# A decoder layer with a mixture of experts: the low parts of the turned rows by a matmul with minus the identity and a ScalarE copy

## What is computed

```python
def moe_ffn(h, w_router, b_router, w_gu, b_gu, w_dn, b_dn):
    ...
    logits = (xf @ w_router + b_router).astype(jnp.float32)
    top_v, top_e = lax.top_k(logits, TOP_K)
    gates = jax.nn.softmax(top_v, axis=-1)
    ...
    def expert_block(args):
        xe, e = args
        gu = xe @ w_gu[e] + b_gu[e]
        gate = jnp.minimum(gu[..., 0::2], SWIGLU_LIMIT)
        up = jnp.clip(gu[..., 1::2], -SWIGLU_LIMIT, SWIGLU_LIMIT)
        act = (up + 1.0) * (gate * jax.nn.sigmoid(gate * SWIGLU_ALPHA))
        return act @ w_dn[e] + b_dn[e]
    ...
    out = jnp.zeros((t, d), jnp.float32).at[row_tok].add(
        yb.reshape(n_rows, d).astype(jnp.float32) * row_gate[:, None])
```

## Time and profile before

| what | us |
| --- | --- |
| median of 3 runs | 1427.1 |
| lowest and highest | 1425.9, 1428.12 |
| the profiled execution, its own time | 1428.16 |
| its span in the profile | 1426.5 |
| busy in the span: PE, DVE, ACT | 1331.1, 1276.3, 1026.1 |

### The profile page before, as it was taken

How to read it: one execution, slowest core, us unless ns; L and a number is a source line. 1 busy time by engine, 2 the same in 40 slices (tenths; PEclk the granted TensorE clock), 3 DMA queues, 4 the chain that set the end, 5 groups by cost and what they waited for, 6 DMA issues and landing times.

```text
span 1426.5 us, 20070 instructions
## 1 busy us (share of the span) xinstructions
PE 1331.1 (93%) x6410; PEld 1058.9 (74%) x6410; DVE 1276.3 (89%) x1246; ACT 1026.1 (72%) x945; POOL 439.6 (31%) x286
## 2 busy tenths in 40 slices
PE   6999989898999999999999999999999999999996
PEld 5876866776877777787877777777878777788883
DVE  7448665689999999999999999999999999999998
ACT  5344444447788888878788888888787888877772
POOL 0000000023143536253444435362535444311100
PEclk9999999999999999999999999999999999999998
DMA  9511130279999999999999999999999999999994
GB/s 352 192 59 60 35 133 31 83 264 382 378 395 403 402 393 406 409 403 405 406 406 400 402 394 404 397 401 406 403 398 400 408 397 396 390 380 374 364 372 178
DMA packets 85573, 472.83 MB, mean 331 GB/s; under 512 B 16619, under 2 KB 16659, under 8 KB 34336
## 3 DMA queue, kind: packets, MB, share of 16 engines
q1 hardware_dynamic: 70736, 451.79, 79.6%
q0 software_dynamic: 14800, 20.55, 4.1%
HBM read 467.80 MB, written 22.02 MB: 343 GB/s over the span
## 4 chain that ended last, share of the span: by engine, by line
PE 50%; DVE 22%; issue 13%; DMA 7%; ACT 6%; POOL 0%; DVEq 0%; SPq 0%; POOLq 0%; ACTq 0%
DVE w_lo L1004 11%; PE gu_bank L1536 10%; PE gu_bank L1538 9%; PE gu_bank L1537 9%; DMA raw<-in_w_down_dram 5%; ACT w_hi L645 4%; PE turn_bank L1536 3%; PE turn_bank L1537 3%; PE turn_bank L1538 3%; DVE arena L1384 2%; PE bank L1536 1%; PE bank L1538 1%; PE bank L1537 1%; PE bank L1861 1%; DVE arena L1394 1%
## 5 line engine op out<-in xcount | busy, mean ns | idle before, releaser
L1004 DVE TENSOR_TENSOR w_lo<-raw,w_hi 128x2048 fp32r<-128x2048 f32 x409 | 916.4, 2283 | 61.1 <-ACT w_hi L645 60.1
L645 ACT ACTIVATE w_hi<-raw 128x2048 fp32r<-128x2048 f32 x409 | 771.9, 1921 | 120.7 <-PE gu_bank L1538 96.2
L610 POOL DMA_INDIRECT expert_rows<-arena x32 | 215.9, 6747 | 303.7 <-ACT arena L831 147.7
L1536 PE MATMUL gu_bank<-w_hi,turned 128*128 128x512 f32 x624 | 246.6, 395 | 3.8 <-DVE w_lo L1004 3.7
L1538 PE MATMUL gu_bank<-w_hi,turned 128*128 128x512 f32 x624 | 243.3, 390 | 0.0
L1537 PE MATMUL gu_bank<-w_lo,turned 128*128 128x512 f32 x624 | 243.1, 390 | 0.0
L1542 PE MATMUL gu_bank<-w_hi,turned 128*128 128x512 f32 x448 | 180.0, 402 | 29.2 <-DVE w_lo L1004 27.9
L1543 PE MATMUL gu_bank<-w_lo,turned 128*128 128x512 f32 x448 | 175.1, 391 | 0.0
L1536 PEld LDWEIGHTS gu_bank<-w_hi,turned 128*128 128x128 f32 x624 | 117.2, 188 | 33.6 <-DVE w_lo L1004 6.6
L584 POOL COPY arena<-arena 128x1 int32 (+1 forms) x32 | 53.0, 1657 | 285.7 <-PE bank L1854 275.1
L1538 PEld LDWEIGHTS gu_bank<-w_hi,turned 128*128 128x128 f32 x624 | 117.1, 188 | 24.8
(11 more groups left out here) (343 smaller groups left out, 1786.4 us busy)
## 6 DMA issues: line engine op xcount, KB each, us to landing
raw<-in_w_gate_up_dram SPq DMA_DIRECT2D x264, 1024.0 KB, 9.5
raw<-in_w_down_dram SPq DMA_DIRECT2D x132, 1024.0 KB, 8.4
raw<-in_w_in_dram SPq DMA_DIRECT2D x10, 1024.0 KB, 7.2
raw<-in_w_out_dram SPq DMA_DIRECT2D x4, 1024.0 KB, 5.1
raw<-expert_rows SPq DMA_DIRECT2D x4, 1024.0 KB, 6.5
turned<-split_biases POOLq DMA_DIRECT2D x132, 4.0 KB, 6.7
raw<-in_w_mem_kv_dram SPq DMA_DIRECT2D x2, 1024.0 KB, 12.5
arena<-in_x_dram SPq DMA_DIRECT2D x1, 2048.0 KB, 13.9
```

The lines of the kernel that those rows point to most:

```text
L610: pool.indirect_dma_start(y_dram, bass.IndirectOffsetOnAxis(idx_scatter, 0), y_row, None, bounds_check=TOPK * S - 1, oob_is_err=False).the ...
L645: a.activation(home, raw_ap, ACT.Copy).then_inc(hi_ready, halves)
L1004: v.tensor_tensor(home[1], raw_ap, home[0].bitcast(F32), ALU.subtract).then_inc(lo_ready, halves)
L1536: pe.matmul(bank, a[0], b[0], start=first, stop=False)
```

## The change

Only iterations W and N change, that is the 14 pairs. PE no longer leaves the turned rows in PSUM as they are. Once ACT has copied the high parts out, PE multiplies them with minus the identity and adds the result in PSUM, so that the low parts stand there (`rest_of_x`, `rest_of_acts`, two matmuls each). ACT then copies them out (`low_x`, `low_act`, two instructions each), and the four pairs of subtractions leave DVE. `rest_of_acts` stands between g3 and g4 on PE, `rest_of_x` between d0 and d1 (in N behind `fold_gate_up`). On ACT `low_act` stands behind one more `hi_m` after `turn_act`, and `low_x` behind one more `hi_m` after `turn_x`. The transposes of both kinds are now written as matmuls that clear a bank only at its first piece. `wide_after_wide` and the last iteration keep the subtractions on DVE.

```diff
@@ ACT @@
+            def low_x(n, rows=P):
+
+                low = lx[:, :, :] if rows == P else hx[:, :, NARROW_ROWS:P]
+                a.wait_ge(x_rest, n)
+                for q in range(2):
+                    ks = slice(4 * q, 4 * q + 4)
+                    a.activation(low[:, ks, :], turned_rows[:, ks, 0:rows], ACT.Copy).then_inc(xlo_ready, 1)
+
+            def low_act(n, rows=P):
+
+                low = la[:, :, :] if rows == P else ha[:, :, NARROW_ROWS:P]
+                a.wait_ge(act_rest, n)
+                for q in range(2):
+                    ks = slice(4 * q, 4 * q + 4)
+                    a.activation(low[:, ks, :], turned_rows[:, ks, 0:rows], ACT.Copy).then_inc(alo_ready, 1)
...
+            a.activation(minus_one, ident, ACT.Copy, scale=-1.0)
...
                 turn_act_narrow(0, b)
                 turn_act_narrow(1, b)
-                for i in range(7, 12):
+                hi_m(GU + 7, b)
+                low_act(b, NARROW_ROWS)
+                for i in range(8, 12):
                     hi_m(GU + i, b)
...
-                for i in range(12, 16):
+                hi_m(GU + 12, b)
+                low_x(b, NARROW_ROWS if narrow_next else P)
+                for i in range(13, 16):
                     hi_m(GU + i, b)
                 low_of_down(b * 12 + (16 + GU))
...
                 turn_act(0, b)
                 turn_act(1, b)
-                for i in range(7, 11):
+                hi_m(GU + 7, b)
+                low_act(b)
+                for i in range(8, 11):
                     hi_m(GU + i, b)
...
                 hi_m(GU + 12, b)
+                low_x(b)
                 sigmoid(b + 1, NARROW_ROWS)
@@ DVE @@
                     lo_m(GU + i, b)
-                turn_act(0, b * 2)
-                turn_act(1, b * 2 + 1)
                 for i in range(7, 12):
                     lo_m(GU + i, b)
-                turn_x(0, b * 2 + 3)
-                turn_x(1, b * 2 + 4)
                 clamp(b + 1, folded)
@@ PE @@
+            def rest_of_x(n, rows=P):
+
+                pe.wait_ge(xhi_ready, n * 2 + 4)
+                for q in range(2):
+                    ks = slice(4 * q, 4 * q + 4)
+                    ins = pe.matmul(turned_rows[:, ks, 0:rows], minus_one, hx[:, ks, 0:rows], start=False, stop=True,
+                                    skip_group_check=True)
+                ins.then_inc(x_rest, 1)
+
+            def rest_of_acts(n, rows=P):
+
+                pe.wait_ge(ahi_ready, n * 2 + 1)
+                for q in range(2):
+                    ks = slice(4 * q, 4 * q + 4)
+                    ins = pe.matmul(turned_rows[:, ks, 0:rows], minus_one, ha[:, ks, 0:rows], start=False, stop=True,
+                                    skip_group_check=True)
+                ins.then_inc(act_rest, 1)
...
                     if k == 2:
                         turn_acts(b)
+                    if k == 3:
+                        rest_of_acts(b)
...
                     if j == 0:
                         fold_gate_up(n)
+                        rest_of_x(b)
```

More of the change, by code:

```diff
@@ L283, in hymba_layer @@
         ha, la = (R[:, i * D:(i + 1) * D].rearrange("p (k s) -> p k s", k=KT) for i in (2, 3))
+        minus_one = R[:, 7 * D:7 * D + P]
         ones_r = R[:, 7 * D + P:7 * D + 2 * P]
@@ L321, in hymba_layer @@
         x_kept = sem("x_kept")
+        x_rest, act_rest = sem("x_rest"), sem("act_rest")
         ones_ready, bias_saved, bias_now_in = sem("ones_ready"), sem("bias_saved"), sem("bias_now_in")
@@ L1368, in turn_x_narrow @@
                                 high.bitcast(F32), ALU.subtract).then_inc(xlo_ready, 1)
[L1370 to L1374, removed]
             def clamp(n, folded=None):
@@ L1439, in wide_after_wide, with wide_after_narrow @@
                     lo_m(GU + i, b)
-            def wide_after_narrow(b, narrow_next):
+            def wide_after_narrow(b):
                 for i in range(4, 7):
                     lo_m(GU + i, b)
-                turn_act_narrow(0, b * 2)
-                turn_act_narrow(1, b * 2 + 1)
                 for i in range(7, 11):
@@ L1450, in wide_after_narrow @@
                 lo_m(GU + 11, b)
[L1451 to L1455, removed]
                 activate(b + 1, b)
@@ L1477, in _ @@
             with v.Fori(1, NARROW) as n:
-                wide_after_narrow(n * 2, True)
+                wide_after_narrow(n * 2)
                 narrow_after_wide(n * 2 + 1, n + 1)
-            wide_after_narrow(LOOP_FROM - 2, False)
+            wide_after_narrow(LOOP_FROM - 2)
             wide_after_wide(LOOP_FROM - 1)
@@ L1853, in turn_rows @@
                 for k in range(KT):
-                    ins = pe.transpose(psum[6 + k // 4][:, k % 4 * P:(k % 4 + 1) * P],
-                                       h_row[:, k * P:(k + 1) * P], ident)
+                    ins = pe.matmul(psum[6 + k // 4][:, k % 4 * P:(k % 4 + 1) * P], h_row[:, k * P:(k + 1) * P], ident,
+                                    start=k % 4 == 0, stop=True, is_transpose=True, skip_group_check=True)
                 ins.then_inc(xtp_done, 1)
+            def rest_of_x(n, rows=P):
[12 more added lines that the diff above has]
+                ins.then_inc(act_rest, 1)
             def turn_acts(n):
@@ L1860, in turn_acts @@
                 for k in range(KT):
-                    ins = pe.transpose(psum[6 + k // 4][:, k % 4 * P:(k % 4 + 1) * P],
-                                       act_by_slice[:, k, :], ident)
+                    ins = pe.matmul(psum[6 + k // 4][:, k % 4 * P:(k % 4 + 1) * P], act_by_slice[:, k, :], ident,
+                                    start=k % 4 == 0, stop=True, is_transpose=True, skip_group_check=True)
                 ins.then_inc(atp_done, 1)
@@ L1909, in wide_after_wide, with wide_after_narrow @@
                     down(j, 2 * GU + j, b)
-            def wide_after_narrow(b):
+            def wide_after_narrow(b, rows_next=NARROW_ROWS):
                 pe.wait_ge(sig_ready, b)
@@ L1918, in wide_after_narrow @@
                         turn_acts(b)
+                    if k == 3:
+                        rest_of_acts(b, NARROW_ROWS)
                 gu_bias(b)
@@ L1924, in wide_after_narrow @@
                     down(j, 2 * GU + j, b, narrow=True)
+                    if j == 0:
+                        rest_of_x(b, rows_next)
             def narrow_after_wide(b, n, between=None):
@@ L1950, in _ @@
                 narrow_after_wide(b, n + 1)
-            wide_after_narrow(LOOP_FROM - 2)
+            wide_after_narrow(LOOP_FROM - 2, P)
             wide_after_wide(LOOP_FROM - 1, NARROW)
```

## The result

| kernel | median us | runs | ratio to the kernel before, 95% interval |
| --- | --- | --- | --- |
| before | 1426.5 | 5 | |
| changed | 1469.7 (1469.0 to 1472.1) | 5 | 1.0304 (1.0291 to 1.0316) |

The five runs of the kernel before include the three of the table ahead of the prediction. The change makes the kernel 43 us slower, 3.0%. The direction was forecast, the size was not: 1457 was named, and the range ended at 1468.

What follows compares the result with a forecast made beforehand. PE's critical stretch and its waits for ACT's gapless run were taken to bound the pair: 1.85 + 0.3 = 2.15 us a pair, 28 over 13 periods, plus 1.0 and 1.1, sum 30; 1427.1 + 30 = 1457, range 1424 to 1468.

Steps and rivals of the forecast that it cites:

- The walk through the pair: Late pair of the profile retimed with the new order, place by place in W and N: 2.15 us more a pair.
- 2, ACT's run from sigmoid to the end of `turn_act`: ACT's run: `low_x` adds 0.52 us and a slot wait 0.1; `turn_act` ends at 731.2 instead of 730.5.
- 3, wait ahead of `rest_of_acts` in N: N, ahead of g4: PE waits from 730.55 to 731.25 for `turn_act`, does 0.55 us; g7 is 1.13 late.
- 4, wait ahead of `rest_of_x` in N: N, ahead of d1: PE waits 0.35 us, does 0.55; d1 2.06 late, 1.85 after the slack of 0.2.
- The sum: 1.85 + 0.3 = 2.15 us a pair, 28 over 13 periods, plus 1.0 at the start and about 1.1 at the end.
- The lower bound of the range: Forecast case at its least: no extra start, narrow passes free, two waits shorter by half; 1.0 us a pair, 1441.
- waits 3 and 4: PE's waits in N for ACT, ahead of g4 (until 731.25) and ahead of d1 (0.35 us).
- step 1: W, ahead of d1: PE stands 2.5 us for `turn_x_narrow`, does 0.3; what remains is covered by the wait for `low_of_down`.
- the clock falls: Rival: the 2.5 us wait halves PE's clock for d1 and d2 of W; 4 us a pair, 1485 and more; 0.06 with costlier passes.
- A granted clock below 1.00 in the pairs: Sign of being wrong: PE's granted clock in the pairs, 1.00 in all windows before, dropping below that.
- DVE is the bound, and its relief wins: Rival: subtractions leaving DVE's chain shorten the pair by 1.0 us, 1413, down to 1385; chance 0.14.
- The waits cover each other: Rival: added PE work and copies fall into PE's three existing waits of 3.4 us; 1427, within 3 us; chance 0.10.

Runs made afterwards that it cites:

- the kernel with the filler: Changed kernel plus nine matmuls with zeros on PE behind d0 in iteration W, ahead of `rest_of_x`; 1453.0 us, ratio 1.0179.
- the run with the wait moved: Changed kernel with `rest_of_x` of iteration W behind d1 instead of d0 and `low_x` behind one more `hi_m`; 1468.0 us, ratio 1.0285.
- the kernel with the wait alone: Kernel before, with PE only waiting behind d0 of iteration W until `turn_x_narrow` is done, no work added; 1436.9 us, ratio 1.0070.
- the x rows of W alone: Kernel before with only the x rows of iteration W changed, the other three places keeping DVE's subtractions; 1436.1 us, ratio 1.0064.

## Why the prediction was wrong in size

*That PE and ACT, not DVE, set the pairs once the matmuls wait:* right. The chain of the changed kernel gives PE 67% of the span (50% before) and DVE 9% (22%).

*The walk through the pair:* right within 0.4 us. It gave 67.4 us; pairs at the full clock take 67.07 to 67.34. The waits came out as forecast or shorter. Its terms, forecast and measured:

| step | forecast | measured |
| --- | --- | --- |
| 1, PE's wait ahead of the narrow `rest_of_x` | 2.5 | 2.32 |
| 1, wait ahead of `fold_down` | 1.2 | 1.10 |
| 2, ACT's run from sigmoid to the end of `turn_act` (17.2 before) | 17.9 | 18.0 |
| 3, wait ahead of `rest_of_acts` in N | 0.7 | 0.43 |
| 4, wait ahead of `rest_of_x` in N | 0.35 | none |
| two matmuls of 512 columns, to the next start | 0.55 | 0.57 |
| work taken from DVE, a pair | 3.7 | 2.9 |
| work added to ACT, a pair | 3.5 | 3.2 |
| two matmuls of 256 columns, to the next start | 0.3 | 0.34 |

The last row also answers the rule of the Trainium skill, page "PSUM — Partial Sum Buffer", on non-contiguous patterns: the narrow matmuls, which write runs of 64 elements, take 0.34 us for two where the contiguous ones of twice the columns take 0.57, so no slowing is seen here.

*The sum:* 24.4 us in the 13 periods (1.9 each), 2.1 at the start and 1.1 at the end give 27.6 us, where the forecast had 28, 1.0 and 1.1. Had the clock held, the time would have been near the 1453.0 of the kernel with the filler, well inside. The lower bound of the range takes 0.35 for half of the waits 3 and 4, which are 0.7 and 0.35; half of them is 0.5, which makes it about 1440 and changes nothing else.

*The step that failed* is a term that the sum of the forecast put at nothing: the price of the clock behind the wait of step 1. The runs show 13.9 us for it, about 1.6 us in nine of 13 periods, which is more than the whole distance from 1457 to 1469.7. The prediction had it only as the rival "the clock falls". It was given a chance of 0.06 together with costlier passes, and the argument against it was that waits of up to 1.5 us leave the clock at 1.00 in the earlier trace rows. That was true of 1.5 us and said nothing of the 2.5 us that step 1 of the same walk had just found. (And ahead of the pairs the same trace has a fall behind a wait of 1.53 us, as told above.) The forecast case should have carried a term for it. The rival's price was wrong too: it doubled d1 and d2, 3.6 us, of which 1.7 was to be covered, so 1.9 us on top of the 2.15 in every pair. The runs show 1.6 us, none of it covered, in nine of 13 periods, since the clock comes back at the start of d2. (Even by its own terms the rival's sum is 1427 + 30 + 13 x 1.9 = 1482, not 1485.) At 0, 4, 9, 10 or 13 falls of 1.6 us the cost is 0 to 21 us, and the likeliest case would have gone from 1457 to 1478. A granted clock below 1.00 in the pairs was among the prediction's own signs of being wrong, and it came.

*The other rivals.* "DVE is the bound, and its relief wins" fell, and for the reason named: g4 stands behind ACT's run. What it missed is that even with those waits moved away, the transfers hold the late pairs. "The waits cover each other" is what happens in the kernel with the wait alone, in the pairs at the full clock (65.2 to 65.7 us), and nearly so with the x rows of W alone (65.4 to 65.7); with all four places moved it does not.

## What to carry to other kernels

An instruction that is moved from a busy engine to one with free time must not make the tensor engine wait in its own order for an engine that runs without a gap: the free share of ACT (17% of a pair) lay elsewhere. When a planned wait of the tensor engine is longer than any that the profile shows at the full clock, give the clock a term of its own in the sum. And when a wait is moved, ask which wait behind it has the same cause: in the run with the wait moved, it got what the first one lost.

## What the runs showed of the chip

- In the pairs PE's clock fell behind waits of 2.3 to 2.4 us and stayed up where all waits were at most 1.9 us. Each fall cost 1.6 us. With nearly the same wait in each pair it came in 4, 9, 10 or 13 of 13, and which ones is open. Outside the pairs the same wait of 2.15 us had a fall behind it in one kernel and none in another.
- Nine matmuls that add zeros, in the place where PE stood still in each W, made the changed kernel 17 us faster (1469.7 to 1453.0).
- Two matmuls of 512 columns with minus the identity, onto transposed rows in PSUM, took 0.57 us to the next start, 0.1 of it behind the wait or the fold; other matmuls of 512 columns take 0.2275 each.
- The transfers held the late pairs of the kernel before, at 395 to 404 GB/s and a share of 0.99 to 1.00: a cut of the gate and up loads by one eighth took 0.3 to 0.6 us off each.
